# One 128x2048 instruction in place of two of 128x1024 in the weight split of a mixture-of-experts kernel

## The reference

```
for each block of 128 tokens of expert e:            # 32 experts, each token goes to 4 of them
    gu = xe @ w_gate_up[e] + b_gate_up[e]             # 1024 -> 2048
    gate, up = split(gu)
    gate = minimum(gate, 7); up = clip(up, -7, 7)
    act = gate * sigmoid(1.702 * gate) * (up + 1)
    y = act @ w_down[e] + b_down[e]                   # 1024 -> 1024
out[token] += routing_weight * y
```

## Time and profile before

| | us |
|---|---|
| median of 3 runs (2427.1 to 2430.07) | 2427.46 |
| the profiled execution | 2427.8 |
| its span, first to last instruction | 2426.2 |
| TensorE busy in the span | 2246.3 |
| VectorE busy | 1752.6 |
| ScalarE busy | 1284.3 |
| the experts' products (L1925), first to last start | 781.8 to 2411.2 |

### The profile page before, as it was taken

One profiled execution on the slowest core, in us unless ns is written; L12 is line 12 of the kernel. 1 busy time (PEld: TensorE's weight loads), 2 busy tenths in 40 slices (PEclk: granted clock), 3 DMA queues, 4 the chain that ended last, 5 costly groups with the idle time before them and its releaser, 6 DMA issues.

```text
span 2426.2 us, 37494 instructions
## 1 busy us (share of the span) xinstructions
PE 2246.3 (93%) x10569; PEld 1817.2 (75%) x10570; DVE 1752.6 (72%) x2230; ACT 1284.3 (53%) x1723; POOL 794.6 (33%) x780
## 2 busy tenths in 40 slices
PE   6899995886972999999999999999999999999997
PEld 2679883775861888888888888878888887878876
DVE  1684424664673699986679967687999768789697
ACT  2332211664322577765567755565777556567575
POOL 1253003893035143342223322231332422133142
PEclk9899997998985999999999999999999999999999
DMA  7134203982232799996669977696999977799695
GB/s 242 64 126 144 69 1 100 257 221 85 105 122 90 276 350 364 378 338 230 223 229 374 366 264 230 225 302 223 375 371 363 317 227 253 271 321 373 239 346 175
DMA packets 299173, 583.98 MB, mean 241 GB/s; under 512 B 23841, under 2 KB 53553, under 8 KB 297009
## 3 DMA queue, kind: packets, MB, share of 16 engines
q1 hardware_dynamic: 269200, 501.68, 59.3%
q0 software_dynamic: 26560, 69.06, 10.5%
q10 hardware_dynamic: 3362, 12.59, 1.4%
HBM read 544.79 MB, written 44.24 MB: 243 GB/s over the span
## 4 chain that ended last, share of the span: by engine, by line
PE 60%; DVE 4%; issue 2%; DVEq 1%; POOL 1%; ACT 0%; DMA 0%; POOLq 0%; ACTq 0%
PE psum L1925 54%; DVE d_wlo L1759 3%; PE psum L1907 3%; PE psum L1869 2%; PE psum L1877 2%; DVE d_up L1772 0%; DVE d_act L1778 0%; DMA d_xg<-xn_d,d_entry 0%; POOL d_colf L1581 0%; DVE d_y_two L1749 0%; ACT d_y_two L1661 0%; DVE d_atlo L1784 0%; DVEq L1445 0%; DVEq L1444 0%; DVEq L1443 0%
## 5 line engine op out<-in xcount | busy, mean ns | idle before, releaser
L1759 DVE TENSOR_TENSOR d_wlo<-d_raw,d_whi 128x1024 fp32r<-128x1024 f32 x578 | 673.7, 1218 | 77.1 <-ACT d_whi L1636 76.1
L1636 ACT ACTIVATE d_whi<-d_raw 128x1024 fp32r<-128x1024 f32 x578 | 574.6, 1053 | 113.1 <-PE psum L1925 88.9
L1925 PE MATMUL psum<-d_whi,d_xthi 128*128 128x512 f32 x1152 | 458.7, 398 | 0.1
L1925 PE MATMUL psum<-d_whi,d_xtlo 128*128 128x512 f32 x1152 | 454.6, 395 | 0.0
L1925 PE MATMUL psum<-d_wlo,d_xthi 128*128 128x512 f32 x1152 | 454.5, 394 | 0.0
L1550 POOL DMA_INDIRECT out_dram<-d_yst,d_dest x49 | 93.0, 1897 | 808.8 <-DVE d_yst L1806 752.1
L1759 DVE TENSOR_TENSOR d_wlo<-slab,d_whi 128x1024 fp32r<-128x1024 f32 x292 | 343.4, 1217 | 4.2 <-ACT d_whi L1636 2.4
L1636 ACT ACTIVATE d_whi<-slab 128x1024 fp32r<-128x1024 f32 x292 | 292.5, 1054 | 6.0 <-PE psum L1925 5.6
L1925 PEld LDWEIGHTS psum<-d_whi,d_xtlo 128*128 128x128 f32 x1152 | 216.9, 188 | 50.7
L1925 PEld LDWEIGHTS psum<-d_whi,d_xthi 128*128 128x128 f32 x1152 | 217.0, 188 | 49.9 <-issue 1.5
L1925 PEld LDWEIGHTS psum<-d_wlo,d_xthi 128*128 128x128 f32 x1152 | 217.3, 189 | 48.4
(11 more groups left out here) (304 smaller groups left out, 3964.4 us busy)
## 6 DMA issues: line engine op xcount, KB each, us to landing
slab<-in_w_gate_up_dram SPq DMA_DIRECT2D x144, 1024.0 KB, 7.6
d_raw<-in_w_gate_up_dram SPq DMA_DIRECT2D x144, 1024.0 KB, 9.0
d_raw<-in_w_down_dram SPq DMA_DIRECT2D x144, 1024.0 KB, 6.9
b_wp<-in_w_ada_dram POOLq DMA_DIRECT2D x16, 1024.0 KB, 8.6
slab<-in_w_in_dram SPq DMA_DIRECT2D x12, 1024.0 KB, 5.4
slab<-in_w_ada_dram SPq DMA_DIRECT2D x8, 1024.0 KB, 5.1
b_q<-q_d SPq DMA_DIRECT2D x24, 256.0 KB, 7.7
b_k<-k_d SPq DMA_DIRECT2D x24, 256.0 KB, 8.6
```

The source lines that it names most:

```text
L1636: nc.scalar.activation(whi[n % NW][:, part, :], raw[n % NRAW][:, part, :], ACT.Copy).then_inc(whi_ok, 1)
L1759: nc.vector.tensor_tensor(wlo[n % NW][:, part, :], raw[n % NRAW][:, part, :], whi[n % NW][:, part, :].bitcast(F32), ALU.subtract).then_inc ...
L1925: mm = nc.tensor.matmul(to, m_[:, KH * h + k, :], w_[n % NW][:, k, :], start=(h == 0 and k == 0 and q == 0), stop=(h == 1 and k == KH - 1 ...
```

## The change

The two quarters of a half slab are handled by one instruction of 128x2048 on ScalarE and one on VectorE. ScalarE makes both waits for the place ahead of its instruction, and the instruction counts `whi_ok` by 2 at its end. VectorE waits for both counts and counts `wlo_ok` by 2 at its end. TensorE's waits and the loads' waits stay as they are written. Nothing else is altered, and the lists of the engines keep their order.

```diff
 # ScalarE, split(g, n)
                     act.wait_ge(raw_in[n % NRAW], 32 * g + 16 * (n // NRAW) + 16)
                     for q in range(2):
-                        part = slice(2 * q, 2 * q + 2)
                         wait_for_slot(act, g, n, q)
-                        nc.scalar.activation(whi[n % NW][:, part, :], raw[n % NRAW][:, part, :],
-                                             ACT.Copy).then_inc(whi_ok, 1)
+                    nc.scalar.activation(whi[n % NW][:, :, :], raw[n % NRAW][:, :, :], ACT.Copy).then_inc(whi_ok, 2)
 # VectorE, split(g, n)
-                    for q in range(2):
-                        part = slice(2 * q, 2 * q + 2)
-                        dve.wait_ge(whi_ok, 2 * NH * g + 2 * n + q + 1)
-                        nc.vector.tensor_tensor(wlo[n % NW][:, part, :], raw[n % NRAW][:, part, :],
-                                                whi[n % NW][:, part, :].bitcast(F32), ALU.subtract).then_inc(wlo_ok, 1)
+                    dve.wait_ge(whi_ok, 2 * NH * g + 2 * n + 2)
+                    nc.vector.tensor_tensor(wlo[n % NW][:, :, :], raw[n % NRAW][:, :, :],
+                                            whi[n % NW][:, :, :].bitcast(F32), ALU.subtract).then_inc(wlo_ok, 2)
```

## The result

The changed kernel takes 2438.62 us (median; 2433.4 to 2441.91), the kernel before 2427.46 (2426.32 to 2431.77). The ratio is 1.004, with a 95% interval of 1.0029 to 1.0052: it is slower by 11 us. The profiled execution took 2438.43 us, its span is 2436.8.

What follows compares the result with a forecast made beforehand. TensorE was taken as the bound, so VectorE's and ScalarE's savings win little. 14.1 us at second turns less 5.8 already lost, plus 0.6 at the end, gives 8.9 us: 2436.4 us, range 2431 to 2446.

Steps and rivals of the forecast that it cites:

- What bounds the kernel: In the experts' stage TensorE is busy nearly throughout, lacking 7.94 of 1635 us; savings on VectorE and ScalarE win little.
- The lengths: A split of a whole half slab takes 2.28 us on VectorE and 1.91 us on ScalarE.
- The shift of the chain: Between the turns of a one-block group, VectorE starts 0.86 us later, saves 0.14; `d_act` ends 0.72 us later.
- The loss per group: TensorE waits 0.59 us at the second turn in all 24 one-block groups, 14.1 us together.
- The room of 0.13 us: At the second turn of a one-block group, the chain can come 0.13 us later before TensorE loses time.
- The seven groups that waited already: Seven one-block groups already lose 5.8 us at the second turn; afterwards they lose 0.59 us each, net +8.3 us.
- At nothing: Two-block groups, weights for TensorE, loads and `d_xtlo` behind the second turn were to cost nothing or little.
- The end: At the end of the experts, the whole copy delays TensorE and the last output and store: +0.6 us.
- The sum: Over the whole kernel, 8.3 + 0.6 = 8.9 us slower, 2436.4 us or +0.37%.
- GpSimd late: Rival, 0.18: longer VectorE instructions delay GpSimd's store and token gather in one-block groups, 9.6 us more, 2440 to 2450.
- The chain moves less: Rival, 0.14: merged copy near elements alone, so the chain to the second turn shifts little; 2425 to 2431 us.
- faster: Rival, 0.06: VectorE's saving shrinks its backlog, the seven waits at the turn vanish and none arises; 2421.7 us.

## Why the prediction was right, by its steps

**What bounds the kernel.** Right. Both engines have less work (0.6 and 0.8 us in a group) and the time rose. Only TensorE's wait at one turn counted.

**The lengths.** 2.28 and 1.91 us were forecast from the middle between 1024 and 3072 elements, 2.288 and 1.915 were measured. The saving of 0.14 us for two splits in a row came out as 981.75 - 977.34 = 4.41 us against 4.55.

**The shift of the chain.** Forecast 0.72 us, measured 9.87 - 9.09 = 0.78. The difference is a step that I took as fixed: the handover. Read off the instructions' own ends, VectorE started 0.03 us behind the quarter that it waited for in the kernel before, and starts 0.10 us behind the whole copy now (977.24 to 977.34). With these 0.07 us the forecast's 0.72 would have been 0.79.

**The loss per group.** Forecast 0.59 us, measured 37.26 - 36.58 = 0.68. The chain gives 0.78 - 0.13 = 0.65 of it. The other 0.03 us is not in every group: from the product behind the second turn to the next group, the 24 groups take 0.16 us more in all. The room of 0.13 us, read from the products' starts, held: a chain of 9.13 us cost nothing, one of 9.49 cost 0.29 us.

**The seven groups that waited already.** Right. Their chain came to the same 9.87 us as in all others, and the forecast's reason for it (the chain is set by ScalarE's copy there too) is what the rows show. This is the term that keeps the loss at +10 in place of +16: 24 x 0.68 = 16.3, less about 6.

**At nothing.** Right for groups of two blocks (no turn in them waits), for TensorE's weights (no wait for `wlo`), for the loads, and for `d_xtlo`. The end was forecast at +0.6 us. In the last group the store, which answers to the earlier trace rows, starts 2425.20 - 2421.0 = 4.2 us behind the yardstick's last product, where it was 2414.16 - 2410.7 = 3.5: +0.7 us. The span ends 15.8 us behind that product, where it was 15.5, so in these two executions 0.3 us of it is left: the last store landed 0.4 us sooner.

```profile
2425.20 1.67 POOL L1550 DMA_INDIRECT out_dram<-d_yst,d_dest  x1 [23.89 <-DVE d_yst L1802]
```

**The sum.** Forecast 8.9 us, measured 11.2 between the medians. For the stage alone the forecast was 8.3, and 10.6 was measured. The handover that was taken as fixed is 24 x 0.07 = 1.7 us of the difference, and it is the mis-sized term. The other 0.6 us lies almost all ahead of the very first turn, in the scatter of that stretch.

**GpSimd late, the rival at 0.18.** It fell, and its reasoning had an error. I took it that GpSimd gets in between any two of VectorE's instructions, so that longer ones would lock it out for longer. The four stores of 5.32 us did not: each ran on beside four subtractions until their row broke. In the changed kernel the row breaks more often, since VectorE waits more for ScalarE's copy. So the stores got shorter: the four of 5.32 us are gone, and the longest takes 3.08. Nor does the loss hang on them. With half slabs 9 and 10 alone whole the four stores of 5.31 to 5.32 us are still there, TensorE waits for no gathered rows behind the stage's start, and the whole loss is there. One of the longer stores of the changed kernel, beside VectorE's row:

```profile
958.87 2.28 DVE L1755 TENSOR_TENSOR d_wlo<-d_raw,d_whi 128x2048 fp32r<-128x2048 f32 x1
961.32 2.29 DVE L1755 TENSOR_TENSOR d_wlo<-d_raw,d_whi 128x2048 fp32r<-128x2048 f32 x1 [0.17 <-ACT d_whi L1635]
...
959.70 2.97 POOL L1550 DMA_INDIRECT out_dram<-d_yst,d_dest  x1 [14.74 <-DVE d_yst L1802]
```

A gap of 0.17 us, at 961.15, was enough: the store ends 1.52 us behind it.

**The chain moves less, and faster.** Both needed a copy well under 1.91 us, and it took 1.915.

## What to carry to other kernels

Before merging two instructions, look at the place where the consumer has nothing in store: there the merge delays the start by the length of the part given up, and saves only what the overlap of neighbours had not hidden already. Here that was 0.78 us lost against 0.07 saved for a half slab, on an engine that wasn't the bound. And where a chain is relieved by moving an instruction ahead, follow every other instruction that thereby comes later, down to the engine that waits for it: the freed 0.8 us came back as a late gather until the output was moved too.

## What the runs showed of the hardware

**A store of GpSimd often waits out a row of VectorE's subtractions.** Behind the first groups of the stage, the kernel before has 4 stores of over 2.5 us, the change 6, and the two kernels with the earlier output 43. In 51 of these 53 the store ends 1.50 to 1.54 us behind the end of a subtraction of VectorE (the other two: 1.31), and in the rows shown so far that is the last subtraction before a break. In these rows the store's length says where in VectorE's row it started: 2.97 us where the gap was near, 5.32 us before, 9.86 us beside eight subtractions. One instruction of another kind is break enough. With the output earlier, the store starts ahead of `d_pick` (VectorE, then GpSimd, whole half slabs):

```profile
997.40 2.28 DVE L1763 TENSOR_TENSOR d_wlo<-d_raw,d_whi 128x2048 fp32r<-128x2048 f32 x1
999.60 0.28 DVE L1817 TENSOR_SCALAR d_pick<-d_rowe,d_colf 128x128 fp32r<-128x128 f32 x1
999.80 2.28 DVE L1763 TENSOR_TENSOR d_wlo<-d_raw,d_whi 128x2048 fp32r<-128x2048 f32 x1
...
998.43 2.78 POOL L1551 DMA_INDIRECT out_dram<-d_yst,d_dest  x1 [14.83 <-DVE d_yst L1811]
```

It ends at 1001.21, 1.53 us behind the subtraction's end at 999.68, although the next one runs from 999.80 on. The Trainium skill (SBUF — State Buffer, "SBUF: two separate sides") says that GpSimd and VectorE share a pair of ports, that whichever of the two starts first holds it for its whole instruction (of VectorE's, one with two SBUF inputs does so only against a GpSimd operation that reads SBUF), and that the other is blocked. The rows agree that the store is held up beside such instructions, and they show a row of them often acting as one.

It is not a rule. In the kernel with whole half slabs and `d_act` earlier, 6 of the 16 long stores behind the first groups end 1.52 to 1.53 us behind a subtraction whose follower comes at the usual overlap of 0.08 us, so that the row had no break. One of them, VectorE and then GpSimd:

```profile
1803.50 6.78 DVE L1763 TENSOR_TENSOR d_wlo<-d_raw,d_whi 128x2048 fp32r<-128x2048 f32 x3 [0.29 <-issue]
...
1803.63 3.70 POOL L1551 DMA_INDIRECT out_dram<-d_yst,d_dest  x1 [16.04 <-DVE d_yst L1811]
```

It ends at 1807.33, inside the row. With ScalarE alone whole, four stores end 1.52 to 1.53 us behind a subtraction whose follower comes only 0.04 us later than usual, with no idle time of VectorE. What decides whether a store waits out the row, the runs don't settle. In all the six, and in one more with half slabs 9 and 10 alone whole, it started 0.11 to 0.14 us behind the start of the row's first subtraction, where those of 5.32 us started 0.83 us behind it.

**Merging two instructions does not save the whole difference of their lengths.** On VectorE that difference is 2 x 1.218 - 2.288 = 0.15 us for one pair, but two pairs in a row save only 4.55 - 4.41 = 0.14 us together, or 0.07 each, since neighbours overlap by 0.08 us.

**The handover from ScalarE to VectorE**, read off the instructions' own ends where VectorE stood idle for the copy, takes in nearly all cases 0.03 us where the waiting subtraction is a quarter, and 0.10 us where it is a whole half slab. The size of the copy waited for doesn't matter: it is 0.03 us with ScalarE alone whole, and 0.10 us with VectorE alone whole. I have no cause for it, and it is 1.7 us of the loss (24 x 0.07).
